# Norms of a two-layer encoder: units around each norm ordered by sequence, mean of squares by a product with ones

## The chip, the cores and the metric

The kernel runs on one core of one Trainium2 chip. The metric is the device time in microseconds of one execution. TensorE does the matrix products, VectorE and ScalarE everything elementwise, GpSimd (POOL) and SyncE issue most of the DMAs. All numbers are float32.

## The reference

Two sequences, of 256 and 512 tokens, go through the same trunk of two layers with 1,024 features; each has its own conditioning vector c. A layer has a mixer and a feed-forward part, and each is fed by a root-mean-square norm that is modulated by c:

```
mod = silu(c) @ w_mod[i] + b_mod[i];  sh1, sc1, g1, sh2, sc2, g2 = split(mod, 6)
h = rmsnorm(x, norm1_g[i]) * (1 + sc1) + sh1
x = x + g1 * mixer(h)              # layer 0: differential attention and gated linear attention; layer 1: mLSTM
h = rmsnorm(x, norm2_g[i]) * (1 + sc2) + sh2
x = x + g2 * ((silu(gate) * up) @ w_down),   gate, up = split(h @ w_gu)
rmsnorm(x, g) = x * rsqrt(mean(x * x) + 1e-6) * g      # mean over the 1,024 features
```

So there are four norms in front of a phase of products (norm 0 before the mixer of layer 0, norm 1 before its feed-forward part, norms 2 and 3 in layer 1) and a last one on the output.

## The kernel before

**Layout.** x, h and all activations lie feature-major: a tile has 128 features in the partitions and 768 columns, the 256 tokens of the first sequence and then the 512 of the second. x has `KD = 8` such tiles. `seq(tile, s)` cuts the columns of sequence s out of a tile: s = 0 is the short one, s = 1 the long one.

**Units.** Every weight matrix is worked off in units of 128 output features (a "feature" unit) or 256 output features with tokens in the partitions (a "token" unit). `plan_units` (L70) puts all units of the kernel in one list; units of one name are a phase. The phases of layer 0 are `bqk0`, `lowrank0`, `bv0`, `aq0`, `ak0`, `bg0`, `av0`, `outb0`, `outa0`, then `gu00`, `down00`, and so on to `down02`; those of layer 1 are `cq1`, `gates1`, `ck1`, `cv1` and `co1`, `out1`, `gu10` to `down12`. The norms stand in front of `bqk0`, `gu00`, `cq1` and `gu10`, behind `outa0` (8 units of 4 k-tiles), `down02` (8 of 6) and `out1` (8 of 8).

**Weights.** Products are made in three parts of a 32-bit operand that is split into a high and a low half: high times high, high times low, low times high. SyncE loads a unit's raw weights into one of four slots as soon as the unit four before it is done (`group_full`); ScalarE copies them to `w_hi` (L1221) and VectorE subtracts to get `w_lo` (L1601). Both do this in `split_to(i)`, which splits all units whose slot was used by a unit up to i. A feature unit is a chain of 3 products per k and per sequence into a pair of banks, 256 columns in the one and 512 in the other (`feature_tile`, L811, products at L824).

**Accumulators.** A pair of banks is free for the next unit when the unit before has been taken out. The phases `gu` and `down` rotate over three pairs, all others over two.

**A norm.** While the phase before runs, VectorE adds each unit's result to x (`residual`, L1737), ScalarE squares the tile (L1278), and VectorE sums the squares (L1667), one tile late. After the last unit TensorE makes the sum over features per token (`norm_sums`, L769): 12 products of the sum and 12 of the last square tile, each with one column of ones, so that tokens lie in the partitions. VectorE scales (L1672, L1673), ScalarE takes the root of 6 columns (L1291), VectorE inverts 6 columns (L1676) and builds six diagonal matrices (L1683), and TensorE broadcasts them over all partitions with a product with ones (L785). Then for each of the 8 tiles and both sequences: `normed` (L1688, VectorE), `h_hi` (L1297, ScalarE), `h_lo` (L1695, VectorE). TensorE runs the first two units of the next phase together, tile by tile as they come (`two_feature_tiles`, L832, products at L842).

**Order.** Each engine's program is one list written by hand; a wait on a semaphore stops all that stands behind it on that engine. At the start, ScalarE copies rows of the modulation out of banks (`mod_row`), splits the first four units, sends x to DRAM (`x_kept`), and goes to norm 0; VectorE splits, completes the modulation of norm 0, makes a table (`band`, L2070) and goes to norm 0. Behind norm 0, VectorE works on further blocks of the modulation (`modulate`, L1617 and L1620, on `early_raw`): GpSimd loads a block when VectorE has freed the buffer of the one two before.

## Time and profile before

| what | value |
| --- | --- |
| three runs | 2117.55, 2123.80, 2126.86 us, median 2123.8 us |
| profiled execution, its own time | 2124.51 us |
| its span, first to last instruction | 2122.4 us |
| mean granted clock of TensorE | 0.967 |
| TensorE busy | 2017.7 us, 95% of the span |
| VectorE busy | 992.6 us, 47% |
| ScalarE busy | 601.7 us, 28% |
| DMA `raw<-in_ffn_w_gu_dram`, 256 KB each | 3.3 us from issue to landing |
| DMA `x_kept<-x`, 3,072 KB each | 10.3 us from issue to landing |

Times are in microseconds from the span's start, durations of single instructions in ns. L824 is line 824 of the kernel. A TensorE instruction's duration holds its way through the array; the spacing of starts is what a product costs. "[3.66 <-DVE h_lo L1695]" means that the engine was idle for 3.66 us before this row and what released it. The granted clock is 1.00 at 2.4 GHz and 0.50 at 1.2 GHz.

### The profile page before, as it was taken

To read this page: it belongs to the slowest core of one execution; us is meant where nothing else is said; L and a number is where in the kernel's file an instruction comes from. 1 tells how busy PE (TensorE), PEld (TensorE's weight loads), DVE (VectorE), ACT (ScalarE), POOL (GpSimd) and SP (SyncE) were. 2 spreads that over 40 slices of the span, in tenths; PEclk is the share of its full clock that TensorE was granted. 3 is DMA by queue.
4 is the path that set the end of the run, shared out by engine and by line. 5 is a ranking of instruction groups with operands and counts; after the bars stand their busy time and mean duration, and the time that the engine had idled before them with its cause. 6 is when DMAs were issued, how large, how long until landed. Compare 5 with 4: busy or idle time off the path is not lost.

```text
span 2122.4 us, 28746 instructions
## 1 busy us (share of the span) xinstructions
PE 2017.7 (95%) x12081; PEld 1742.5 (82%) x12081; DVE 992.6 (47%) x1875; ACT 601.7 (28%) x1101; POOL 74.3 (4%) x121
## 2 busy tenths in 40 slices
PE   7879999988899999999998999998989999999998
PEld 2768888767788888888887788888878888888887
DVE  1877425684766665652235334544452222222224
ACT  3235224652321112211223333334232211211213
POOL 2010000000011101100000000000000000000000
PEclk9889999999899999999998999999989999999999
DMA  7343112012344444432223201021212222222212
GB/s 282 120 150 108 41 41 80 21 31 60 99 142 138 136 122 139 142 96 60 65 62 104 60 20 41 21 99 49 61 50 60 60 70 60 64 66 60 62 56 82
DMA packets 210249, 174.16 MB, mean 82 GB/s; under 512 B 10320, under 2 KB 196792, under 8 KB 208584
## 3 DMA queue, kind: packets, MB, share of 16 engines
q1 hardware_dynamic: 197536, 117.67, 18.5%
q0 software_dynamic: 12288, 48.35, 7.1%
q10 hardware_dynamic: 296, 6.29, 0.7%
q8 instruction: 96, 1.57, 0.3%
q14 instruction: 33, 0.27, 0.0%
HBM read 162.85 MB, written 9.44 MB: 81 GB/s over the span
## 4 chain that ended last, share of the span: by engine, by line
PE 87%; DVE 6%; ACT 4%; issue 2%; DMA 1%; POOL 0%; ACTq 0%; DVEq 0%; POOLq 0%
PE bank L824 60%; PE bank L790 9%; PE bank L842 4%; PE bank L1096 2%; PE bank L747 1%; PE bank L765 1%; DMA early_raw<-in_w_mod_dram 1%; ACT w_hi L1221 1%; DVE early_acc L1620 1%; DVE w_lo L1601 1%; PE bank L1018 1%; PE bank L908 1%; PE bank L1041 1%; PE bank L966 1%; PE bank L1068 1%
## 5 line engine op out<-in xcount | busy, mean ns | idle before, releaser
L824 PE MATMUL bank<-h_hi,w_hi 128*128 128x256 f32 x1600 | 409.4, 338 | 0.1
L824 PE MATMUL bank<-h_lo,w_hi 128*128 128x256 f32 x1600 | 407.5, 336 | 0.0
L824 PE MATMUL bank<-h_hi,w_lo 128*128 128x256 f32 x1600 | 407.3, 336 | 0.0
L1601 DVE TENSOR_TENSOR w_lo<-raw,w_hi 128x1024 fp32r<-128x1024 f32 (+4 forms) x195 | 239.0, 1230 | 340.2 <-ACT w_hi L1221 340.1
L824 PEld LDWEIGHTS bank<-h_hi,w_lo 128*128 128x128 f32 x1600 | 301.3, 188 | 33.6
L824 PEld LDWEIGHTS bank<-h_lo,w_hi 128*128 128x128 f32 x1600 | 301.4, 188 | 33.2
L824 PEld LDWEIGHTS bank<-h_hi,w_hi 128*128 128x128 f32 x1600 | 299.4, 188 | 34.2 <-issue 1.9
L1221 ACT ACTIVATE w_hi<-raw 128x1024 fp32r<-128x1024 f32 (+4 forms) x196 | 205.6, 1053 | 226.3 <-DMA raw<-in_ffn_w_down_dram 129.1
L790 PE MATMUL bank<-w_hi,h_hi 128*128 128x256 f32 x672 | 214.8, 320 | 18.1 <-DVE w_lo L1601 17.7
L790 PE MATMUL bank<-w_lo,h_hi 128*128 128x256 f32 x672 | 195.8, 291 | 0.0
L790 PE MATMUL bank<-w_hi,h_lo 128*128 128x256 f32 x672 | 195.6, 291 | 0.0
L1737 DVE SCALAR_TENSOR_TENSOR x<-bank,mod,x 128x256 f32<-128x256 f32 (+1 forms) x144 | 82.3, 613 | 229.6 <-PE bank L824 225.6
L824 PE MATMUL bank<-act_hi,w_hi 128*128 128x256 f32 x704 | 179.4, 337 | 4.6 <-issue 4.6
L824 PE MATMUL bank<-act_lo,w_hi 128*128 128x256 f32 x704 | 178.8, 336 | 0.0
L824 PE MATMUL bank<-act_hi,w_lo 128*128 128x256 f32 x704 | 178.7, 336 | 0.0
L790 PEld LDWEIGHTS bank<-w_hi,h_hi 128*128 128x128 f32 x672 | 134.5, 200 | 31.0 <-DVE w_lo L1601 18.1
L824 PEld LDWEIGHTS bank<-act_hi,w_hi 128*128 128x128 f32 x704 | 131.7, 188 | 19.8 <-issue 5.8
L824 PEld LDWEIGHTS bank<-act_lo,w_hi 128*128 128x128 f32 x704 | 132.4, 188 | 14.5
L824 PEld LDWEIGHTS bank<-act_hi,w_lo 128*128 128x128 f32 x704 | 132.4, 188 | 14.4
L790 PEld LDWEIGHTS bank<-w_lo,h_hi 128*128 128x128 f32 x672 | 134.6, 200 | 4.9 <-issue 3.8
L790 PEld LDWEIGHTS bank<-w_hi,h_lo 128*128 128x128 f32 x672 | 134.4, 200 | 0.0
L1620 DVE SCALAR_TENSOR_TENSOR late_acc<-late_raw,c_cols,late_acc 128x512 f32<-128x512 f32 x196 | 133.7, 746 | 0.6 <-DMA late_raw<-in_w_mod_dram 0.6
(274 smaller groups left out, 2251.7 us busy)
## 6 DMA issues: line engine op xcount, KB each, us to landing
raw<-in_ffn_w_gu_dram SPq DMA_DIRECT2D x176, 256.0 KB, 3.3
late_raw<-in_w_mod_dram POOLq DMA_DIRECT2D x56, 512.0 KB, 4.3
raw<-in_ffn_w_down_dram SPq DMA_DIRECT2D x64, 256.0 KB, 3.3
early_raw<-in_w_mod_dram POOLq DMA_DIRECT2D x24, 512.0 KB, 4.4
wide<-in_w_mod_dram SPq DMA_DIRECT2D x8, 1024.0 KB, 18.7
raw<-in_odd_w_in_dram SPq DMA_DIRECT2D x16, 512.0 KB, 4.4
raw<-in_even_w_in_dram SPq DMA_DIRECT2D x24, 256.0 KB, 5.0
x_kept<-x ACTq DMA_DIRECT2D x2, 3072.0 KB, 10.3
```

The lines of the kernel that those rows point to most:

```text
L747: last = mm(bank[4 + c][0:2, :], c_cols[:, k, :], wide[k][:, c * 512:(c + 1) * 512], start=(k == 0), stop=(k == KD - 1))
L765: last = mm(mod_column(l, c0 // P + m)[:, s:s + 1], mod_acc(b)[:, s, m * P:(m + 1) * P], ones[:, 0:1], start=True, stop=True)
L790: last = mm(out, stationary[a], moving[b], start=(k == 0 and n == 0), stop=(k == K - 1 and n == 2))
L824: last = mm(pair(u.pair)[s], wk[a], seq(operand(o, k), s), start=(k == 0 and n == 0), stop=(k == u.ks - 1 and n == 2))
L842: last = mm(pair(u.pair)[s], wk[a], seq(operand(o, k), s), start=(k == 0 and n == 0), stop=(k == u.ks - 1 and n == 2))
L908: last = transpose(out[s][:, c:c + P], source(t), ident[:])
L966: last = mm(bank[6][:, d * P:(d + 1) * P], k_e[c][rows, t * P:(t + 1) * P], q_e[c][rows, t * P:(t + 1) * P], start=True, stop=True)
L1096: last = mm(bank[7][:, 0:C_V + 1], weights[d][:, c:c + P], z_cv[:, h, i, :], start=(i == froms[0]), stop=(i == froms[-1]))
L1221: fn(hi, r, ACT.Copy).then_inc(hi_ready, 1)
L1601: v.tensor_tensor(lo, r, hi.bitcast(F32), ALU.subtract).then_inc(unit_split, 1)
L1620: ins = v.scalar_tensor_tensor(acc, mod_raw(m)[:, kk, :], c, acc, ALU.mult, ALU.add)
L1737: last = v.scalar_tensor_tensor(seq(x[:, f, :], s), pair(u.pair)[s], mod[l][:, gate + f, s:s + 1], seq(x[:, f, :], s), ALU.mult, ALU.add)
```

## The change

At norms 1 to 3 the last two units of the phase before (`TAILS`) are worked off by sequence: the long sequence of unit 6 and of unit 7, the short one of unit 6, the sums for the long one, the short one of unit 7. At norms 0 to 3 the first three units of the phase behind (`HEADS`) are: the long sequence of units 0 and 1 together, tile by tile, with the sums for the short one behind the third tile, the long one of unit 2, and then the short one of units 0, 1 and 2. The three have a pair of banks each.

The sum over features is made with the 128 x 128 matrix of ones as the stationary operand and the squares as the moving one, three products for each sequence (the sum of the first six tiles, and the squares of the last two). Each partition then holds the sums of all tokens, in a bank. ScalarE takes the root of mean plus epsilon over the whole row out of the bank into `rstd_all`, VectorE inverts the row in place. The diagonal matrices and their 12 products go, and so do the sums per token, except at the last norm, which stays as it was.

`normed`, `h_hi` and `h_lo` run over the 8 tiles of the long sequence and then over those of the short one. Between them stand, on VectorE, the short residual of unit 7, the two weight splits and the second inversion; on ScalarE, the last square, the second root and two weight splits, and at norms 0 and 2 the DMA of x to DRAM. At norm 0 the sums are made before `turn_rows`, and ScalarE takes both roots ahead of its first weight splits.

The diff, cut to its core:

```diff
-        rstd_diag = at("rstd_diag", Z + 57 * KB, [P, TILES, P])
+        rstd_all = at("rstd_all", Z + 57 * KB, [P, T])
...
+        TAILS = ("outa0", f"down0{FG - 1}", "out1")
+        HEADS = ("bqk0", "gu00", "cq1", "gu10")
...
-            pairs = 3 if base in ("gu", "down") else 2
-            u.pair = (0 if u.n == 0 and pairs == 3 else features) % pairs
+            if u.tail is not None:
+                by = "res"
+                taken["res"] = 4 * u.tail + 2 + u.n - (KD - 2)
+            pairs = 3 if base in ("gu", "down") or u.name in HEADS and u.n < 3 else 2
+            u.pair = u.n if u.name in HEADS and u.n < 3 else (0 if u.n == 0 and pairs == 3 else features) % pairs
...
-        def mean_bank(n):
-
-            return bank[6 if 0 < n < 4 else 0]
+        def mean_of(n, s):
+
+            if n == 0:
+                return pair(0)[s]
+            return bank[6][:] if s else bank[7][:, 256:512]
...
-            def norm_sums(n):
-
-                pe.wait_ge(sq_summed, (KD - 2) * (n + 1))
+            def norm_sums(n, s):
+
+                pe.wait_ge(sq_summed, (KD - 3) * (n + 1))
+                if n == 0:
+                    pe.wait_ge(tr_free, KD)
+                mm(mean_of(n, s), ones[:], seq(square_sum, s), start=True, stop=False)
+                for f in (KD - 2, KD - 1):
+                    pe.wait_ge(sq_ready, 10 * n + (7, 9)[1 - s] + f - (KD - 2))
+                    last = mm(mean_of(n, s), ones[:], seq(square[f % 2], s), start=False, stop=(f == KD - 1))
+                last.then_inc(mean_full, 1)
...
-                for t in range(TILES):
-                    s = SEQ_OF_TILE[t]
-                    c = (t - SEQ_TILES[s][0]) * P
-                    pe.wait_ge(rdiag_ready, TILES * n + t + 1)
-                    mm(pair(2)[s][:, c:c + P], ones[:], rstd_diag[:, t, :], start=True, stop=True).then_inc(rstd_full, 1)
...
+            def tail_units(us, n, operand):
+
+                for u in us:
+                    pe.wait_ge(unit_split, u.i + 1)
+                    wait_free(u)
+                for s in (1, 0):
+                    for u in us:
+                        if s == 0 and u is us[1]:
+                            if n == 2:
+                                pe.wait_ge(mod_ready, 1 + len(MOD_BLOCKS))
+                            norm_sums(n, 1)
+                        for k in range(u.ks):
+                            wk = [slot_of(wt, u)[:, k * P:(k + 1) * P] for wt in (w_hi, w_lo)]
+                            for m, (a, o) in enumerate(((0, 0), (0, 1), (1, 0))):
+                                last = mm(pair(u.pair)[s], wk[a], seq(operand(o, k), s),
+                                          start=(k == 0 and m == 0), stop=(k == u.ks - 1 and m == 2))
+                        last.then_inc(group_full, 1)
+
+            def head_units(us, n):
+
+                def products(u, s, k):
+                    wk = [slot_of(wt, u)[:, k * P:(k + 1) * P] for wt in (w_hi, w_lo)]
+                    for m, (a, o) in enumerate(((0, 0), (0, 1), (1, 0))):
+                        last = mm(pair(u.pair)[s], wk[a], seq(normal(o, k), s),
+                                  start=(k == 0 and m == 0), stop=(k == KD - 1 and m == 2))
+                    return last
+
+                for u in us[:2]:
+                    pe.wait_ge(unit_split, u.i + 1)
+                    wait_free(u)
+                for k in range(KD):
+                    pe.wait_ge(h_ready, 2 * KD * n + k + 1)
+                    for u in us[:2]:
+                        products(u, 1, k)
+                    if n and k == 2:
+                        norm_sums(n, 0)
+                pe.wait_ge(unit_split, us[2].i + 1)
+                wait_free(us[2])
+                for k in range(KD):
+                    products(us[2], 1, k)
+                for u in us:
+                    for k in range(KD):
+                        if u is us[0]:
+                            pe.wait_ge(h_ready, 2 * KD * n + KD + k + 1)
+                        last = products(u, 0, k)
+                    last.then_inc(group_full, 1)
+                for u in us:
+                    after(u)
...
+            pe.wait_ge(row_taken, 4)
+            norm_sums(0, 1)
+            norm_sums(0, 0)
...
+            def mean_root(n, s):
+
+                act.wait_ge(mean_full, 2 * n + 2 - s)
+                fn(seq(rstd_all, s), mean_of(n, s), ACT.Sqrt, scale=1.0 / D, bias=eps_col[:, 0:1]).then_inc(root_ready, 1)
+
             def norm(n, i):
-                act.wait_ge(mean_ready, n + 1)
+
+                def high(f, s):
+                    act.wait_ge(normed_ready, 2 * KD * n + KD * (1 - s) + f + 1)
+                    fn(seq(h_hi[:, f, :], s), seq(normed[f % 2], s), ACT.Identity,
+                       bias=mod[n // 2][:, (SH1, SH2)[i] + f, s:s + 1]).then_inc(h_hi_ready, 1)
+
+                def square_late(f, s, done):
+                    act.wait_ge(res_done, 4 * (n - 1) + done)
+                    square_part(n, f, s)
+
+                if n:
+                    us = phase[TAILS[n - 1]]
+                    split_to(us[KD - 3].i)
+                    fn(dummy[:], ones[:, 0:1], ACT.Sqrt)
+                    square_late(KD - 2, 1, 1)
+                    square_late(KD - 1, 1, 2)
+                    square_late(KD - 2, 0, 3)
+                    mean_root(n, 1)
+                for f in range(KD):
+                    high(f, 1)
+                    if n and f == 1:
+                        square_late(KD - 1, 0, 4)
+                    if n and f == 3:
+                        mean_root(n, 0)
+                        split_to(us[KD - 2].i)
+                if n:
+                    split_to(us[KD - 1].i)
+                if n % 2 == 0:
+                    spill()
+                for f in range(KD):
+                    high(f, 0)
...
+            for s in (1, 0):
+                for q in (KD - 2, KD - 1):
+                    square_part(0, q, s)
             act.wait_ge(mod_full, KD)
             for c in (0, 1):
                 fn(mod_row[:, c * 512:(c + 1) * 512], bank[4 + c][0:2, :], ACT.Copy).then_inc(row_taken, 1)
+            mean_root(0, 1)
+            mean_root(0, 0)
...
+            def inverse(n, s):
+
+                dve.wait_ge(root_ready, 2 * n + 2 - s)
+                link(v.reciprocal(seq(rstd_all, s), seq(rstd_all, s)))
+
+            def norm(n, l, i, gate=None, gate_l=None):
+
+                before = 2 * KD * n
+
+                def part_residual(u, s):
+                    dve.wait_ge(group_full, u.full[s])
+                    v.scalar_tensor_tensor(seq(x[:, u.n, :], s), pair(u.pair)[s], mod[gate_l][:, gate + u.n, s:s + 1],
+                                           seq(x[:, u.n, :], s), ALU.mult, ALU.add).then_inc(res_done, 1)
+
+                def scaled(f, s):
+                    if f >= 2:
+                        dve.wait_ge(h_ready, before + KD * (1 - s) + f - 1)
+                    v.scalar_tensor_tensor(seq(normed[f % 2], s), seq(x[:, f, :], s), gain[l][i][:, f, s:s + 1],
+                                           seq(rstd_all, s), ALU.mult, ALU.mult).then_inc(normed_ready, 1)
+
+                def rest(f, s):
+                    dve.wait_ge(h_hi_ready, before + KD * (1 - s) + f + 1)
+                    v.scalar_tensor_tensor(seq(h_lo[:, f, :], s), seq(normed[f % 2], s),
+                                           mod[l][:, (SH1, SH2)[i] + f, s:s + 1],
+                                           seq(h_hi[:, f, :], s).bitcast(F32), ALU.add, ALU.subtract).then_inc(h_ready, 1)
+
+                dve.wait_ge(mod_ready, (1, 1 + EARLY // MOD_PARTS, 1 + len(MOD_BLOCKS), 1 + len(MOD_BLOCKS))[n])
+                if n:
+                    us = phase[TAILS[n - 1]]
+                    add_squares(n, KD - 3)
+                    split_to(us[KD - 3].i)
+                    part_residual(us[KD - 2], 1)
+                    part_residual(us[KD - 1], 1)
+                    part_residual(us[KD - 2], 0)
+                    inverse(n, 1)
                 for f in range(KD):
-                    if f >= 2:
-                        dve.wait_ge(h_ready, h_before[l, i] + f - 1)
-                    scaled(f)
-                    if f >= 1:
-                        rest(f - 1)
-                rest(KD - 1)
+                    if f == 0:
+                        scaled(0, 1)
+                    if f + 1 < KD:
+                        scaled(f + 1, 1)
+                    rest(f, 1)
+                    if n and f == 0:
+                        part_residual(us[KD - 1], 0)
+                    if n and f == 4:
+                        split_to(us[KD - 2].i)
+                if n:
+                    inverse(n, 0)
+                for f in range(KD):
+                    if f == 0:
+                        scaled(0, 0)
+                    if f + 1 < KD:
+                        scaled(f + 1, 0)
+                    rest(f, 0)
+                    if n and f == 1:
+                        split_to(us[KD - 1].i)
...
+            inverse(0, 1)
+            inverse(0, 0)
             norm(0, 0, 0)
```

## Rows read from the trace of the kernel before

**Rows 1.** The page, busy time of each engine:

```profile
PE 2017.7 (95%) x12081; PEld 1742.5 (82%) x12081; DVE 992.6 (47%) x1875; ACT 601.7 (28%) x1101; POOL 74.3 (4%) x121
```

**Rows 2.** Waits of TensorE: us in total, times, longest:

```profile
PE bank L790 <- DVE w_lo L1601: 17.7, 2, 12.6
...
PE bank L842 <- DVE x L1737: 1.4, 1, 1.4
```

**Rows 3.** Timeline at the fourth norm: start, us, engine, line, operation, idle before:

```profile
1539.87 1.14 DVE L1737 SCALAR_TENSOR_TENSOR x<-bank,mod,x 128x256 f32<-128x256 f32 x2 [3.38 <-PE bank L824]
...
1547.64 2.19 DVE L1688 SCALAR_TENSOR_TENSOR normed<-x,gain,bank 128x256 f32<-128x256 f32 x4 [2.04 <-PE bank L785]
...
1551.27 0.98 PE L842 MATMUL bank<-h_hi,w_hi 128*128 128x256 f32 x2 [3.66 <-DVE h_lo L1695]
```

**Rows 4.** Windows: stretch, busy PE PEld DVE ACT POOL, granted clock, DMA:

```profile
1552.00:1556.00 4.00, 4.00 (x14) 3.37 (x13) 3.93 (x8) 2.24 (x4) 0.00 (x0) 0.50 0.00 0
```

**Rows 5.** Timeline, takers of the units that bound the fourth, third and second norm:

```profile
1522.91 1.14 DVE L1737 SCALAR_TENSOR_TENSOR x<-bank,mod,x 128x256 f32<-128x256 f32 x2 [3.38 <-PE bank L824]
...
1579.12 0.88 ACT L1322 ACTIVATE silu_g<-bank 128x256 f32<-128x256 f32 x2 [3.47 <-PE bank L824]
...
1111.80 1.14 DVE L1737 SCALAR_TENSOR_TENSOR x<-bank,mod,x 128x256 f32<-128x256 f32 x2 [1.62 <-PE bank L824]
...
1164.23 0.87 ACT L1254 ACTIVATE z_o<-bank 128x256 f32<-128x256 f32 x2 [6.65 <-PE bank L824]
...
521.75 1.14 DVE L1737 SCALAR_TENSOR_TENSOR x<-bank,mod,x 128x256 f32<-128x256 f32 x2
...
562.86 0.38 ACT L1322 ACTIVATE silu_g<-bank 128x256 f32<-128x256 f32 x1 [2.86 <-PE bank L842]
```

**Rows 6.** Timeline of TensorE, two spacings of products and the plain f32 ones:

```profile
1530.24 0.40 PE L824 MATMUL bank<-odd_hi,w_hi 128*128 128x512 f32 x1
...
1530.47 0.52 PE L824 MATMUL bank<-odd_lo,w_hi 128*128 128x256 f32 x2
...
42.51 7.03 PE L747 MATMUL bank<-wide,c_cols 128*2 128x512 f32 x16
```

**Rows 7.** Groups by form: count, busy us, mean ns, idle before:

```profile
L1688 DVE SCALAR_TENSOR_TENSOR normed<-x,gain,bank 128x512 f32<-128x512 f32 x32 | 23.8, 742 | 0.0
...
L1601 DVE TENSOR_TENSOR w_lo<-raw,w_hi 128x1024 fp32r<-128x1024 f32 x148 | 180.4, 1223 | 268.8 <-ACT w_hi L1221 268.8
...
L1297 ACT ACTIVATE h_hi<-normed,mod 128x512 fp32r<-128x512 f32 x32 | 22.7, 708 | 0.0
```

**Rows 8.** Groups by form, the reciprocals of VectorE:

```profile
L1868 DVE RECIPROCAL recip<-denom 128x2 f32<-128x2 f32 x24 | 3.8, 159 | 0.0
...
L1676 DVE RECIPROCAL mean_sq<-mean_sq 128x6 f32<-128x6 f32 x5 | 1.0, 192 | 1.4 <-ACT mean_sq L1291 1.4
...
L1716 DVE RECIPROCAL rstd<-rstd 128x24 f32<-128x24 f32 x1 | 0.3, 304 | 0.9 <-ACT rstd L1303 0.9
```

**Rows 9.** Windows, an idle spell and what follows it:

```profile
1484.00:1488.00 4.00, 0.83 (x5) 0.75 (x6) 2.15 (x3) 2.73 (x3) 0.00 (x0) 1.00 0.92 251
...
1488.00:1492.00 4.00, 4.00 (x16) 3.43 (x15) 2.15 (x4) 1.79 (x2) 0.00 (x0) 0.59 0.05 14
```

**Rows 10.** Timeline at the first norm and up to the token unit:

```profile
50.55 3.88 ACT L1221 ACTIVATE w_hi<-raw 128x1024 fp32r<-128x1024 f32 x4
...
50.91 1.32 PE L754 MATMUL bank<-ident,mod_row 2*128 2x2 f32 x16 [1.37 <-DVE mod_row L2064]
...
57.46 1.09 DVE L2070 SCALAR_TENSOR_TENSOR band<-band 128x896 f32<-128x896 f32 x1
...
62.76 2.19 DVE L1688 SCALAR_TENSOR_TENSOR normed<-x,gain,bank 128x256 f32<-128x256 f32 x4 [2.05 <-PE bank L785]
...
80.84 0.88 DVE L1617 TENSOR_SCALAR early_acc<-early_raw,c_cols 128x512 f32<-128x512 f32 x2
...
125.27 2.28 DVE L1601 TENSOR_TENSOR w_lo<-raw,w_hi 128x2048 fp32r<-128x2048 f32 x1
```

More of the change, by code:

```diff
@@ L859, in feature_units @@
+            def feature_units(name, before=None, operand=normal, mix=None, head=None, tail=None):
                 us = phase[name]
+                if head is not None:
+                    head_units(us[:3], head)
+                    us = us[3:]
                 if before:
@@ L1548, in _ @@
             run(phase["outb0"], take_nothing, mix)
[L1549 removed]
+            run(phase["outa0"][:-2], squares_of(1), mix)
             norm(1, 1)
             feed_forward(0)
[L1552 removed]
             norm(2, 0)
```

157 lines of the change are left out of this document (71 added, 86 removed).

## The prediction

> **What bounds the kernel now.** I read the page's first part first: TensorE is busy for 95% of the span, so the time is the products plus the few places where they stop [rows 1]. Second the waits of TensorE: the longest single one, 12.6 us, is not at a norm at all but at the first token unit of the even layer, for a `w_lo` of VectorE; a second row shows what two accumulator pairs cost when a pass needs both free at its start, 1.4 us [rows 2]. Third the timeline around one norm (the fourth, before `gu10`). VectorE takes up the last unit at 1539.87; the sums, the root, the diagonal and the broadcast products follow, `normed` starts at 1547.64, and the first product of the next phase at 1551.27. The products ended 0.2 us before VectorE started, so the gap is 1551.27 - 1539.67 = 11.6 us [rows 3]. Fourth the clock by windows: half (1.2 of 2.4 GHz) at 1552 to 1556, with TensorE busy again [rows 4]. It stayed so for some 5.5 us of products, worth about 2.5 us.
>
> I measure a norm from the end of unit 5 of the phase before (the third last) to the end of unit 2 (the third) of the phase behind, since all that is moved lies between. Each end is 0.2 us before the row of its taker. Last norm: 1522.91 to 1579.12, 56.2 us. Third: 1111.80 to 1164.23, 52.4. Second: 521.75 to 562.86 for unit 0, and then one k of unit 1 (1.1) and unit 2 (8.5) less the taker's 0.2, 50.5 [rows 5].
>
> **Unit prices.** A product of 512 columns takes 0.235 us (1530.24 to 1530.47, rounded), and units 6 and 7 of `out1` took (1539.87 - 1522.91) / 48 = 0.353 for a pair of 256 and 512 [rows 3, 5], so 256 take 0.12. I take it that the parts cost no more when ordered by sequence, since each product is an instruction of its own already; the bound the other way, 512 columns at 0.26, would cost 1 us a norm. The sums' operands are plain f32: 16 of 512 columns in 7.03 us, 0.43 each [rows 6]. VectorE: 0.74 us for 512 columns; an `x` of 256 and 512 takes 1.14 [rows 3], so 256 alone about 0.48; two in a row without a wait overlap by 0.08; a split of a unit 1.22. ScalarE: 0.71 for an `h_hi` of 512; for the root of 512 out of a bank I take 0.65 [rows 7].
>
> **The new operation: a reciprocal over whole rows.** `rstd` is now taken in every partition, and VectorE inverts 512 and 256 columns at each norm where it inverted 6. The trace has no wide one. Two columns take 159 ns, six 192, 24 take 304 [rows 8]. From 6 to 24 that is 6.2 ns a column: 0.30 + 488 x 0.0062 = 3.34 us for 512, and 1.75 for 256. Upper bound, the slope from 2 to 6, 8.2 ns: 4.3 and 2.2. Lower bound: as fast as any other 512 (0.74 and 0.48). I take the first, as it is the same instruction over the widest step, and 18 more columns at the pace of the 512s could have cost only 0.02 us. It speaks against the change either way. The Trainium skill (VectorE: DVE Perf Modes, "First, the fixed hardware budget") says that reciprocal is an iterative divide "with a repeat count of 8". If that is eight steps a column at the pace of the 512 rows (1.03 ns), it would be about 4.4 and 2.3 us, an estimate by that page, and the sum below would end at 2133; the row of 24 columns bears out six steps, the one of six columns eight.
>
> **Last norm, step by step** (from the end of unit 5 as 0). The pass over units 6 and 7 asks for both accumulators at its start, and unit 7's belongs to unit 5: the 1.4 us of [rows 2], new here and at the second norm; the third has three pairs and none. Long sequence of unit 6 (24 x 0.235) to 7.0, of unit 7 to 12.7, short one of unit 6 to 15.6, three sums to 16.9, short one of unit 7 to 19.7. Beside it: VectorE adds unit 7's long part to x from 12.9, ScalarE squares it by 14.3, so the sums don't wait. Root from 17.1 to 17.7, reciprocal to 21.1, `normed` 0.74, `h_hi` 0.71, `h_lo` 0.74 with their handovers to 23.4. The first two units ask for both pairs at their start, and unit 7's short residual (0.5) stands behind the first `h_lo` on VectorE, so the first product is at 24.0. The gap is 4.3 us instead of 11.6, and 24 small sums and 12 broadcast products are gone.
> Then the head. VectorE's period for the long sequence is 0.74 - 0.08 + 0.74 + 0.03 = 1.44 us a k, and TensorE's for two units 6 x 0.235 = 1.41: with nothing to spare, all that VectorE and ScalarE do in between is paid. Besides that residual it is the root of the short sequence, for which ScalarE waits on sums that TensorE issues behind k = 2, and then a `w_hi` of 1.05, which make `h_hi` 4 late by about 1.7, and the `w_lo` split behind `h_lo` 4 (1.2). TensorE idles 3.1 us in k 1 to 7 and, with its sums (0.65), ends the long pass at 39.0. Unit 2's long part to 44.7. VectorE meanwhile inverts the short sequence (1.75) and runs 8 periods of 0.91 with a split; TensorE waits 0.5 for it, and unit 2 ends at 53.9. So 29.9 us from the first product; before it was 27.6 of which 2.5 clock. Total 53.9 for 56.2: 2.3 gained.
> Third norm: tail 14.1 (short tiles of 6), gap 5.0, head 29.9: 48.9 for 52.4, 3.5 gained. Second: tail 11.5 with the stall, gap 5.7 (the last short part of 4 k hides less), head 29.9: 47.0 for 50.5, 3.5 gained.
>
> **Clock.** Idle spells of some 3 us in this trace are followed by a few us at half clock: the window 1484 to 1488 has 0.83 us of products, and 1488 to 1492 has a granted clock of 0.59, 1.7 us lost [rows 9]. Each new gap is of that size. In the head 1.7 us of loss is partly eaten by TensorE's later waits on VectorE; stepping through it, 1.2 stay. The waits inside the head may bring a second such spell: a half chance of 1.2, 0.6. So 1.8 a norm. The three norms gain 9.3 - 5.4 = 3.9 us (bounds: 9.3 without any loss, about -1 where both spells come in full at each, 3.4 a norm).
>
> **First norm.** Nothing precedes it but the row copies, so only losses are in reach. ScalarE's root now stands ahead of its four weight splits. TensorE starts the six sums at 50.9, when the rows are copied; 1.95 us at full clock, 3.3 with most at half, and with handover and root ScalarE is free at about 54.9, where its splits began at 50.55 [rows 10]: 4.3 later, and VectorE's splits with them. VectorE's band work ended at 58.55 and `normed` began at 62.76, 4.2 us; now two reciprocals stand there, 5.2: 1.0. The eight k took 18.2 us to 80.9; now 8 x 1.44 + 8 x 0.91 with the start, 20.2: 2.1. Sum 7.4, say 7.5. TensorE's own path would lose about 4, but it doesn't set the end: behind the norm VectorE runs its modulation blocks from 80.84 in one chain, each needing the buffers the last one freed, up to the `w_lo` that ends at 127.55, for which TensorE waits 12.6 us [rows 2, 10]. All of the 7.5 is passed on. Bounds: 3.6 (reciprocal cheap) to 9. The spill of x (10.3 us to land by the page) moves behind the long pass, is issued at about 80 and lands before unit 0 is full at about 93: nothing, with 2 us of cover.
>
> **Sum.** 2124.5 (profiled execution; 0.7 above the median of the three runs) + 7.5 - 3.9 = 2128.1, on the median's scale 2127.
>
> **Rivals.**
> A, wide reciprocal as cheap as any other 512: the first norm costs 3.6, the others gain 3.1 more each (2.6 at the gap, 0.5 in the short pass), 13.2: 2124.5 + 3.6 - 13.2 = 2115, 2114 on the median's scale. The slope speaks against it.
> B, no clock loss: each gap is under half of the old one and the granted clock stays at 1: 9.3 - 7.5, 2122. Rows 9 speak against it, but such spells are few.
> C, slower: the head starved by VectorE. TensorE waits k by k in the long pass, and the clock falls twice per norm: once with the 2.5 us of the old gap, once more with 1.4. That is 3.9 against the 3.1 gained, 0.8 lost at each of three norms: 2124.5 + 7.5 + 2.4 = 2134. It decides as soon as two half-clock spells follow one norm. For it: 1.44 against 1.41. Against: TensorE never rests over 2 us at a time inside the head.
> D, reciprocal at the steeper slope: 1.0 and 0.5 more at each of four norms, 6 in all: 2133. The row of 24 columns is against it. (It is what the page of the Trainium skill named above would give.)
> E, the first norm's delay is taken up by the 12.6 us wait, if that wait has another cause (the DMA of the modulation blocks running on its own time): only TensorE's 4, 2124.
>
> **Chances.** Forecast (2124 to 2131) 0.45, A 0.11, B 0.14, C 0.11, D 0.09, E 0.10. Half a per cent is 10.6 us and is about what a measurement of this kernel can tell: under 2113 is A with some luck, 0.14; over 2134 is C, or C with D, 0.16; 0.70 within. Range 2114 to 2137: A's centre to C and D together.
>
> **What would show it.** `RECIPROCAL rstd_all` of 512 at 3.3 us (A: 0.7, D: 4.4). First product of `gu10` 24 us after unit 5's end, unit 2's end 54 to 55.5 after it. `h_hi` 4 late by a `w_hi` at every norm but the first. The first modulation block at about 88.3 instead of 80.84, and the first L790 product at about 135 instead of 127.6. It would be wrong if the 12.6 us wait shrinks by the delay, if the clock stays full through the gaps, or if the tail's both-accumulators stall isn't there.

## The result, and the profile after

| | before | after |
| --- | --- | --- |
| median of the timed runs | 2124.08 us (5 runs, 2117.55 to 2126.86) | 2136.57 us (5 runs, 2133.82 to 2140.5) |
| profiled execution, its span | 2124.51, 2122.4 us | 2133.82, 2132.1 us |
| mean granted clock | 0.967 | 0.976 |

The ratio is 1.006, 95% interval 1.0039 to 1.008. Ten more runs of the changed kernel gave 1.0043 (1.0022 to 1.0064). So the change costs 9 to 13 us; forecast were 3. The five runs before were on the quick side: 31 later runs of the same kernel have a median of 2127.99 us. The page of the changed kernel, busy time of each engine, stands against [rows 1]:

```profile
PE 2010.2 (94%) x11985; PEld 1722.7 (81%) x11985; DVE 1005.0 (47%) x1844; ACT 609.8 (29%) x1113; POOL 74.3 (3%) x121
```

TensorE is busy for 7.5 us less and still ends later. The waits of TensorE (us in total, times, longest) answer to [rows 2]:

```profile
PE bank L894 <- DVE h_lo L1811: 21.9, 7, 15.0
PE bank L808 <- DVE w_lo L1712: 15.9, 2, 10.9
PE bank L894 <- DVE x L1800: 14.5, 3, 5.5
```

L894 holds the head's products, L808 the token units'. "Long" and "short" stand for the sequences of 512 and of 256 tokens, a "taker" is the first instruction on VectorE or ScalarE that reads a finished unit out of its banks, and tiles are counted from 0, so that `h_lo` 4 is the fifth. The token unit still waits 10.9 us for `w_lo`, 1.7 less than before, of a delay of 7.7. The groups by form on VectorE (count, busy us, mean ns, idle before) have the new operation, against [rows 8]:

```profile
L1792 DVE RECIPROCAL rstd_all<-rstd_all 128x512 f32<-128x512 f32 x4 | 13.4, 3353 | 8.5 <-ACT rstd_all L1372 8.4
...
L1792 DVE RECIPROCAL rstd_all<-rstd_all 128x256 f32<-128x256 f32 x4 | 7.0, 1747 | 0.0
```

The timeline of the changed kernel at the first norm, against [rows 10]:

```profile
53.35 0.69 ACT L1372 ACTIVATE rstd_all<-bank,eps_col 128x512 f32<-128x512 f32 x1 [1.85 <-PE bank L791]
...
54.64 0.47 ACT L1372 ACTIVATE rstd_all<-bank,eps_col 128x256 f32<-128x256 f32 x1 [0.61 <-PE bank L791]
55.02 3.88 ACT L1292 ACTIVATE w_hi<-raw 128x1024 fp32r<-128x1024 f32 x4
...
61.93 1.09 DVE L2208 SCALAR_TENSOR_TENSOR band<-band 128x896 f32<-128x896 f32 x1
63.05 5.14 DVE L1792 RECIPROCAL rstd_all<-rstd_all 128x512 f32<-128x512 f32 x2
68.23 1.42 DVE L1806 SCALAR_TENSOR_TENSOR normed<-x,gain,rstd_all 128x512 f32<-128x512 f32 x2
...
135.29 0.58 PE L808 MATMUL bank<-w_hi,h_hi 128*128 128x256 f32 x1 [10.85 <-DVE w_lo L1712]
```

ScalarE's splits start at 55.02 instead of 50.55, `band` ends at 63.02 instead of 58.55, the inversions take 5.14, and the first token product comes at 135.3 where it came at 127.6.

The timeline of the changed kernel at the fourth norm, against [rows 3]; unit 5 ends at 1528.63:

```profile
1530.12 0.47 PE L885 MATMUL bank<-odd_hi,w_hi 128*128 128x512 f32 x1 [1.33 <-DVE x L1874]
...
1543.98 1.02 PE L788 MATMUL bank<-square_sum,ones 128*128 128x512 f32 x2
1544.84 1.88 PE L791 MATMUL bank<-square,ones 128*128 128x512 f32 x4
1546.15 0.68 PE L885 MATMUL bank<-odd_hi,w_hi 128*128 128x256 f32 x1
...
1547.47 3.35 DVE L1792 RECIPROCAL rstd_all<-rstd_all 128x512 f32<-128x512 f32 x1 [2.81 <-ACT rstd_all L1372]
...
1553.65 0.77 PE L894 MATMUL bank<-h_hi,w_hi 128*128 128x512 f32 x1 [4.07 <-DVE x L1800]
...
1556.78 0.63 PE L894 MATMUL bank<-h_lo,w_hi 128*128 128x512 f32 x1
1557.20 0.63 PE L894 MATMUL bank<-h_hi,w_lo 128*128 128x512 f32 x1
...
1560.44 0.59 PE L788 MATMUL bank<-square_sum,ones 128*128 128x256 f32 x2
...
1561.93 0.47 ACT L1372 ACTIVATE rstd_all<-bank,eps_col 128x256 f32<-128x256 f32 x1 [5.51 <-PE bank L791]
...
1563.99 0.75 DVE L1811 SCALAR_TENSOR_TENSOR h_lo<-normed,mod,h_hi 128x512 fp32r<-128x512 f32 x1 [5.43 <-ACT h_hi L1378]
```

Read it from below. VectorE stands for 5.43 us before the fifth `h_lo`. It waits for ScalarE, which stands 5.51 us before the short root. That waits for TensorE's short sums at 1560.44. They stand behind three tiles of products, and TensorE comes to them 6.8 us after the first head product (1553.65), since its products of 512 columns start 0.42 apart here (1556.78, 1557.20) and not 0.235. The windows of the changed kernel (columns as in rows 4) show it, with a granted clock of 0.55 and 0.60 up to the sums and of 1.00 behind them:

```profile
1552.00:1556.00 4.00, 2.35 (x6) 1.90 (x7) 3.84 (x7) 2.48 (x5) 0.00 (x0) 0.55 0.19 56
1556.00:1560.00 4.00, 4.00 (x13) 3.16 (x12) 2.49 (x4) 0.42 (x1) 0.00 (x0) 0.60 0.02 4
1560.00:1564.00 4.00, 3.28 (x15) 2.44 (x13) 0.01 (x1) 2.07 (x4) 0.00 (x0) 1.00 0.00 0
```

The rows of the sums show one thing more. The program asks for three products (one of `square_sum`, two of `square`), and the trace has six records: a product with plain f32 operands leaves two (L747 has 64 records in the kernel before, for the 32 products that the program asks for). Six records at 0.43 us (0.86 for the first two, 1543.98 to 1544.84) are 2.6 us, and the short sums take half of that, 1.3 us. So the 24 small sums and 12 broadcasts of a norm that stand above as products are records too; the kernel before has 12 and 6 products.

From unit 5's end, in us, at norms 1, 2 and 3 (before: 50.5, 52.4 and 56.2 in all):

| norm | first head product | from there to the end of unit 2 | in all | VectorE's wait before `h_lo` 4 |
| --- | --- | --- | --- | --- |
| 1 | 18.15 | 31.7 | 49.9 | 4.58 |
| 2 | 20.19 | 31.6 | 51.8 | 4.62 |
| 3 | 25.02 | 32.6 | 57.6 | 5.43 |

**Where the 9.7 us between the two spans are.** First norm, up to the first token product: +7.7. The three norms: -0.6, -0.6, +1.4. The stages between: +1.8, with both signs in them, from -4.2 in the odd layer's mixer to +5.9 in the feed-forward part of layer 0 (norm 1's unit 2 to unit 5 of `down02`); in the latter the slow pace of 576 to 695 and from 911 us on, told below, is worth about 6. No instruction was added there. The takers of the `gu1` units show what changed. The timeline of ScalarE in the kernel before:

```profile
1629.05 0.88 ACT L1322 ACTIVATE silu_g<-bank 128x256 f32<-128x256 f32 x2 [5.41 <-PE bank L824]
1645.68 0.88 ACT L1322 ACTIVATE silu_g<-bank 128x256 f32<-128x256 f32 x2 [5.41 <-PE bank L824]
```

and in the changed one:

```profile
1620.36 0.87 ACT L1432 ACTIVATE silu_g<-bank 128x256 f32<-128x256 f32 x2 [5.57 <-PE bank L842]
1637.32 0.87 ACT L1432 ACTIVATE silu_g<-bank 128x256 f32<-128x256 f32 x2 [5.57 <-PE bank L842]
```

Two units, 48 pairs of 256 and 512 columns, take 16.63 us before and 16.96 after, at a granted clock of 1.00 in both; by the starts of TensorE's products that is 0.3467 and 0.3533 us a pair. These are two paces of one instruction stream; over all pairs, the excess over 0.3467 (called the excess from here on) adds up to 3.5 us in the profile before and 10.2 in the one after. The experiments ask whether that belongs to the change.

### The profile page after: what moved, and what is told of

It is laid out like the page before. It is cut to its first block and busy times, and to the rows that moved or that the text cites. A ratio compares the mean times of both kernels' runs of the same rounds, so it can differ in the third digit from the quotient of the medians.

```text
span 2132.1 us, 28543 instructions
## 1 busy us (share of the span) xinstructions
PE 2010.2 (94%) x11985; PEld 1722.7 (81%) x11985; DVE 1005.0 (47%) x1844; ACT 609.8 (29%) x1113; POOL 74.3 (3%) x121
## 5 line engine op out<-in xcount | busy, mean ns | idle before, releaser
L842 PE MATMUL bank<-h_hi,w_hi 128*128 128x256 f32 (+1 forms) x1536 | 395.6, 339 | 0.2 <-ACT z_bv L1333 0.2
L842 PE MATMUL bank<-h_hi,w_lo 128*128 128x256 f32 (+1 forms) x1536 | 395.2, 339 | 0.0
L842 PE MATMUL bank<-h_lo,w_hi 128*128 128x256 f32 (+1 forms) x1536 | 395.0, 339 | 0.0
L842 PEld LDWEIGHTS bank<-h_hi,w_lo 128*128 128x128 f32 x1536 | 290.4, 189 | 34.4
L842 PEld LDWEIGHTS bank<-h_lo,w_hi 128*128 128x128 f32 x1536 | 290.6, 189 | 32.7
L842 PEld LDWEIGHTS bank<-h_hi,w_hi 128*128 128x128 f32 x1536 | 288.8, 189 | 34.3 <-issue 1.4
L808 PE MATMUL bank<-w_hi,h_hi 128*128 128x256 f32 x672 | 212.5, 316 | 16.4 <-DVE w_lo L1712 15.9
L808 PE MATMUL bank<-w_lo,h_hi 128*128 128x256 f32 x672 | 193.9, 288 | 0.0
L808 PE MATMUL bank<-w_hi,h_lo 128*128 128x256 f32 x672 | 193.5, 288 | 0.0
L842 PE MATMUL bank<-act_hi,w_hi 128*128 128x256 f32 (+1 forms) x680 | 174.5, 338 | 4.6 <-issue 4.6
L842 PE MATMUL bank<-act_hi,w_lo 128*128 128x256 f32 (+1 forms) x680 | 174.0, 338 | 0.0
L842 PE MATMUL bank<-act_lo,w_hi 128*128 128x256 f32 (+1 forms) x680 | 172.7, 336 | 0.0
L808 PEld LDWEIGHTS bank<-w_hi,h_hi 128*128 128x128 f32 x672 | 132.3, 197 | 28.9 <-DVE w_lo L1712 16.3
L808 PEld LDWEIGHTS bank<-w_lo,h_hi 128*128 128x128 f32 x672 | 132.4, 197 | 4.8 <-issue 3.8
L1436 ACT ACTIVATE act_hi<-prod 128x768 fp32r<-128x768 f32 x44 | 37.2, 846 | 335.2 <-DVE prod L1894 335.2
```

The source lines that it names most:

```text
L808: last = mm(out, stationary[a], moving[b], start=(k == 0 and n == 0), stop=(k == K - 1 and n == 2))
L842: last = mm(pair(u.pair)[s], wk[a], seq(operand(o, k), s), start=(k == 0 and n == 0), stop=(k == u.ks - 1 and n == 2))
L1436: fn(act_hi[:, j, :], prod[:], ACT.Copy).then_inc(act_hi_ready, 1)
```

## The experiments

The theory at this point had four parts: (1) which pace holds is drawn anew each time TensorE starts again, and that explains the scatter of the runs; (2) the first norm's loss is the roots ahead of the splits; (3) the norms' loss is the short root, which waits for sums that TensorE reaches late at half clock; (4) the inversion costs its full length at each norm. All ratios are to the kernel before on the same chip, with 95% intervals; the intervals reach about 0.2%, 4 us, to either side, so a smaller difference between two variants can be read from the traces alone.

**The changed kernel once more.** No edit.

> The changed kernel, unaltered, for a second profile. In the first profile the pair of a 256- and a 512-column product in the feed-forward part of layer 0 starts every 0.3533 us in 577 to 696 and again in 911 to 1122, and every 0.3467 in between, while the kernel before has 0.3467 throughout; that accounts for about 5.9 us of the 9.3 between the two profiled executions. Theory 1 (the pace is drawn anew each time TensorE starts after an idle spell): this profile has the slow pace in other phases than the first, and the time moves by up to 10 us with it. Theory 2 (the pace belongs to the order of the program): the same phases are slow within a few us. Ratio to the kernel before 1.004 to 1.008 either way.

1.0043 (1.0022 to 1.0064). First token product 135.7, norms 49.7, 51.8, 56.4, waits before `h_lo` 4 of 4.4, 4.6, 4.2: the same. The pace was slow in other stretches (fast from 918 to 1177 us, slow from 500 to 918), as the first theory has it. The excess was 9.6 us in all against 10.2, and yet the span was 2.3 us longer (2134.4), so the pace isn't the whole of the scatter.

**Roots of the first norm behind the splits.**

```diff
-            mean_root(0, 1)
-            mean_root(0, 0)
             split_to(-1)
+            mean_root(0, 1)
+            mean_root(0, 0)
```

> At norm 0 alone ScalarE takes its two roots behind the four weight splits instead of ahead of them. Theory (norm 0's delay is passed on whole through VectorE's chain of modulation blocks): the band work ends 4.3 us earlier, the first modulation block starts at about 83.4 instead of 87.65 and the first token product at about 131 instead of 135.3: 4 us less than the changed kernel. Rival (the chain runs on the DMA of the blocks): the first token product stays within 1 us of 135.3 and the time is unchanged.

The timeline of this kernel:

```profile
50.61 3.88 ACT L1292 ACTIVATE w_hi<-raw 128x1024 fp32r<-128x1024 f32 x4
55.80 1.05 ACT L1372 ACTIVATE rstd_all<-bank,eps_col 128x512 f32<-128x512 f32 x2
...
58.64 5.14 DVE L1792 RECIPROCAL rstd_all<-rstd_all 128x512 f32<-128x512 f32 x2
...
129.94 0.58 PE L808 MATMUL bank<-w_hi,h_hi 128*128 128x256 f32 x1 [13.30 <-DVE w_lo L1712]
```

The splits are back at 50.6 and the token product comes 5.35 us sooner: part 2 holds in the trace, and the wait for `w_lo` is 13.3 us, so it hides next to nothing of a delay. The ratio did not move: 1.0042 (1.0023 to 1.006). In the profile the gain is still there at unit 5 before the fourth norm (1522.9 against 1528.6) and gone at the end (span 2135.6): the slow pace held to the end, where the changed kernel's first profile was fast from 1699 us on, which is worth 8 of the 9 us. The excess was 18.2 us in all. Whether that was so in most of the ten runs is not known.

**Short root and split two tiles later.**

```diff
-                    if n and f == 3:
+                    if n and f == 5:
                         mean_root(n, 0)
```

(and VectorE's split behind `h_lo` 6 instead of 4)

> At norms 1 to 3 ScalarE's root of the short sequence and the weight split behind it move from behind the fourth h_hi to behind the sixth, VectorE's split from behind the fifth h_lo to behind the seventh. Theory (ScalarE waited for sums that TensorE reached late at half clock, 4.6 to 5.4 us of VectorE's idle time before the fifth h_lo at each norm): that wait goes to under 0.5 us, and from the first product of the head to the end of its third unit it takes 29 to 30 us instead of 31.7 to 32.6: 2 to 3 us a norm, 6 to 9 in all. Rival (TensorE at half clock is itself the limit of the head, the wait only reflects it): the wait moves to h_lo 7, and under 1 us a norm is gained.

1.0009 (0.9982 to 1.0036). Norms 48.0, 49.5, 54.6; the first head products where they were (18.16, 20.18, 25.01). 7.1 us gained behind them, as part 3 says. But the wait was expected to fall under 0.5 us, and 2.4 to 2.8 stay, now before `h_lo` 6. The timeline names what it is:

```profile
1551.46 0.59 PE L788 MATMUL bank<-square_sum,ones 128*128 128x256 f32 x2
...
1552.96 0.47 ACT L1372 ACTIVATE rstd_all<-bank,eps_col 128x256 f32<-128x256 f32 x1 [2.64 <-PE bank L791]
...
1555.02 0.75 DVE L1811 SCALAR_TENSOR_TENSOR h_lo<-normed,mod,h_hi 128x512 fp32r<-128x512 f32 x1 [2.56 <-ACT h_hi L1378]
```

**The same, and TensorE's short sums one tile sooner.**

```diff
-                    if n and k == 2:
+                    if n and k == 1:
                         norm_sums(n, 0)
```

> The short root and the weight split behind h_hi 5 and 6 of the long sequence, as in the run that placed them late, and the short sequence's sums after k = 1 of the head instead of k = 2. Theory (what is left of the wait before h_lo 6, 2.4 to 2.8 us, is TensorE at half clock reaching the sums: two units by three products by 0.43 us for each k): the sums come 2.6 us earlier, the wait before h_lo falls under 0.6 us at each norm, and the norms are 1 to 2.5 us shorter than with the late root alone (48.0, 49.5, 54.6 us): 46 to 47, 47 to 48.5 and 52.5 to 53.5; the time 2124 to 2129. Rival (the wait is the root's table or the residual's square, not TensorE's place): the wait stays at 2 to 3 us and the time at 2130.

1.0003 (0.9986 to 1.0021), norms 46.3, 48.2, 52.8. The timeline of this kernel at norm 1, and at norm 3 with no idle time before the root:

```profile
552.84 0.75 DVE L1811 SCALAR_TENSOR_TENSOR h_lo<-normed,mod,h_hi 128x512 fp32r<-128x512 f32 x1 [0.36 <-ACT h_hi L1378]
...
1553.31 0.59 PE L788 MATMUL bank<-square_sum,ones 128*128 128x256 f32 x2
...
1554.80 0.48 ACT L1372 ACTIVATE rstd_all<-bank,eps_col 128x256 f32<-128x256 f32 x1
```

No wait over 0.4 us is left before an `h_lo`. So the wait, and what it costs, are shown: two moves, with no work taken away, bring 11 to 12 us of the norms (147.3 in all three, against 159.3 and 157.9 in the two profiles of the changed kernel). By the ratios the time fell by 0.4% of the changed kernel's, some 8 us (median 2130.6, where 2124 to 2129 were expected). The 4.9 us of the second move don't show in the time (1.0009 and 1.0003), and the intervals are too wide to tell.

**Without the inversion.** `reciprocal` becomes a multiplication by 0.02 of the same shape; the norm is then not computed, so this is a bound and no version.

> The inversion of the root over whole rows is left out at norms 0 to 3: a multiplication by a constant of the same shape stands in its place (the norm is not computed any more). Theory: 3.35 and 1.75 us become about 0.5 and 0.3, so norm 0 ends 4.3 us earlier on VectorE and passes that on to the first token product (131 instead of 135.3), and each other norm gains 2.8 at the gap and up to 1 behind: 12 to 15 us less than the changed kernel, ratio to the kernel before 0.999 to 1.001. Rival (the head is bound by its own products and waits): under 6 us in all.

0.9958 (0.9937 to 0.9978), 18 us under the changed kernel. In its timeline the operation takes 0.43 us:

```profile
1534.84 0.43 DVE L1792 TENSOR_SCALAR rstd_all<-rstd_all 128x512 f32<-128x512 f32 x1 [2.81 <-ACT rstd_all L1372]
```

This kernel also settles how much of the wait before `h_lo` 4 is the clock's. At its fourth norm TensorE ran at full clock (granted clock 1.00 from 1536 to 1544), with the short sums still behind the third tile:

```profile
1538.10 0.47 PE L894 MATMUL bank<-h_hi,w_hi 128*128 128x512 f32 x1 [1.15 <-DVE x L1800]
...
1542.29 0.59 PE L788 MATMUL bank<-square_sum,ones 128*128 128x256 f32 x2
...
1545.85 0.75 DVE L1811 SCALAR_TENSOR_TENSOR h_lo<-normed,mod,h_hi 128x512 fp32r<-128x512 f32 x1 [2.84 <-ACT h_hi L1378]
```

The sums come 4.2 us behind the first head product and the wait is 2.84. In the changed kernel they come 5.9, 5.8 and 6.8 behind it, and the waits are 4.58, 4.62 and 5.43 (4.38, 4.58 and 4.18 in its second profile). At the other two norms of this kernel the granted clock was 0.73 and 0.72 up to the sums and the waits 4.26 and 4.61, so leaving out the inversion doesn't shorten them. Part 3 as it stood is half of the truth: the place behind three tiles makes 2.8 us of the wait at full clock, and the half clock adds 1.3 to 2.6.

Each first head product comes 2.9 us sooner (15.19, 17.27, 22.11), the first token product at 130.3 (5.0 sooner), the norms take 46.0, 48.3, 51.5. Part 4 holds. The time fell by more than the 12 to 15 us expected; the trace adds up to 18.5, in which the full clock at the fourth norm has its share.

**The order alone.** Sums per token, narrow root and reciprocal, diagonals and broadcast products as before the change; the order by sequence stays, and the first norm's roots stand behind the splits.

```diff
-                link(v.reciprocal(seq(rstd_all, s), seq(rstd_all, s)))
+                link(v.reciprocal(mean_sq[:, ts[0]:ts[-1] + 1], mean_sq[:, ts[0]:ts[-1] + 1]))
+                for t in ts:
+                    v.tensor_scalar(rstd_diag[:, t, :], ident[:], mean_sq[:, t:t + 1], None, ALU.mult).then_inc(rdiag_ready, 1)
```

> The first half of the change alone: the order by sequence stays, the second half is undone (sums per token in single columns, a root over 4 or 2 columns, a reciprocal over 4 or 2 columns, diagonals, and products of ones with the diagonals, issued after the sixth k of the tail's last unit and after k = 1 of the head's third unit; at the first norm the roots stand behind the four weight splits, as before the change). Theory (at norms 1 to 3 the two forms cost about the same, since what the long reciprocal takes on VectorE, 3.35 us, the narrow form takes in 24 weight loads of 0.12, 2.9 against 2.2 us, four diagonals, 0.8, and eight broadcast products, 2.0; the second half costs time at the first norm alone): modulation starts at 81 to 83 us and the first token product at 128 to 130 (135.3 with the change); the three norms 49 to 52, 51 to 54 and 56 to 59 us, the wait before h_lo 4 at 5 to 7 us, since the short sums at half clock are 12 weight loads of 0.22 (2.6 us) against 1.6; the time 2127 to 2134, some 5 under the changed kernel's 2136. Rival (the second half eats the order's gain at the norms too): each of the three norms 3 to 4 us shorter than the changed kernel's, 46, 48 and 53 us, and the time 2116 to 2122.

1.0052 (1.0024 to 1.008), 2140.16: outside what either side expected. First token product 131.8 (not 128 to 130: TensorE now makes the single-column sums, 7.2 us of them mostly at half clock, ahead of the row transposes that VectorE needs). Norms 52.9, 53.6, 59.2, all longer than the changed kernel's. The timeline at norm 3:

```profile
1556.11 0.18 DVE L1822 RECIPROCAL mean_sq<-mean_sq 128x4 f32<-128x4 f32 x1 [2.39 <-ACT mean_sq L1401]
1556.33 0.88 DVE L1824 TENSOR_SCALAR rstd_diag<-ident,mean_sq 128x128 f32<-128x128 f32 x4
...
1558.68 1.80 PE L814 MATMUL bank<-rstd_diag,ones 128*128 128x128 f32 x8
...
1581.94 0.87 DVE L1840 SCALAR_TENSOR_TENSOR normed<-x,gain,bank 128x256 f32<-128x256 f32 x2 [3.43 <-PE bank L814]
```

The narrow inversion saves 3 us on VectorE, and the diagonals, the wait for the place in TensorE's list and four products (eight records) take them back: the first head products come at 18.2, 20.1 and 25.6 us, where the changed kernel has 18.15, 20.19 and 25.02. All that is longer lies behind them; for the short sequence VectorE waits 3.43 us for broadcasts that I had placed behind the third unit's second k. That wait is a mistake of placement in this kernel, not of the form. What can be said: the wide form isn't what makes the norms of the changed kernel slow. The expectation that the two forms cost about the same holds up to the first head product; that the placement alone makes the rest longer is argued and not shown. The ten runs spread from 2131.2 to 2153.7 us, and the profiled one is the slowest.

**Last unit of the attention tails in a third pair of banks.**

```diff
+            if u.tail is not None and u.n == KD - 1 and base != "down":
+                u.pair = 2
```

> The changed kernel with the last unit of the two attention stages (out of norms 1 and 3) in the third pair of banks instead of the second, so that the last two units don't wait for the residual of unit 5. Theory (the stall of 1.4 us at the start of the last two units, seen twice, is on the path): both stalls go, the first head product of norms 1 and 3 comes 1.2 to 1.5 us sooner after unit 5's end (16.8 and 23.6 us against 18.15 and 25.0), the norms are 48.4 and 56.2 us against 49.9 and 57.6, the middle one stays at 51.8, and the time falls by 2 to 4 to 2132 to 2134. Rival (the head waits for VectorE's long pass over the square, the root and the reciprocal, which start from the last residual anyway): the stalls go, and the first head product comes no sooner, or comes sooner by under 0.5 us; the time stays at 2136.

1.0026 (1.0003 to 1.0049). The wait of 1.33 in the timeline at the fourth norm above is gone, the first head products come at 16.99 and 23.08 (1.2 and 1.9 sooner), norm 2 is unchanged at 20.20. The norms take 49.1, 51.8 and 54.8 us, and the stall was on the path. The time doesn't show it: 2137.2 where 2132 to 2134 were expected, and the ratio is within the interval of the changed kernel's.

**The kernel before once more.** No edit.

> The kernel before, unaltered, for a second profile of it. Theory 1 (TensorE takes one of two paces for a pair of 256 and 512 columns, 0.3467 or 0.3533 us, drawn anew whenever it starts again after an idle spell, the same for both kernels): its first profile held the slow pace after the third norm only (3.5 us in all); this one should hold it in other stretches, between 0 and 18 us in all, and its span should move with that sum. Rival (each kernel has its paces fixed by its own order of work): slow again from 1140 us on and nowhere else, 3 to 4 us in all. The first norm (modulation at 80.8, first token product at 127.6) and the three norms (50.5, 52.4, 56.2 us from unit 5's end to the third unit's end) repeat to 0.7 us, but for the spells at half clock, by either.

Span 2128.8, 6.4 us over its first profile; the first norm was the same (modulation at 80.90, token product at 127.5), and the excess over the fast pace was 10.0 instead of 3.5, 6.5 us more. The timeline of ScalarE in it, two neighbouring takers of `gu0` units, with two units and the sums of a modulation block between them:

```profile
775.18 0.88 ACT L1322 ACTIVATE silu_g<-bank 128x256 f32<-128x256 f32 x2 [13.67 <-PE bank L824]
793.92 0.88 ACT L1322 ACTIVATE silu_g<-bank 128x256 f32<-128x256 f32 x2 [7.35 <-PE bank L824]
```

and in its first profile:

```profile
769.21 0.88 ACT L1322 ACTIVATE silu_g<-bank 128x256 f32<-128x256 f32 x2 [13.52 <-PE bank L824]
787.64 0.88 ACT L1322 ACTIVATE silu_g<-bank 128x256 f32<-128x256 f32 x2 [7.20 <-PE bank L824]
```

18.74 and 18.43 us for the same work of the same kernel. The excess went up by what the span did. So the pace is no property of the program alone, and that much of part 1 holds; that the whole scatter comes of it isn't shown. Nor is it free of the program. Behind norms 1 and 3 (600 to 680 and 1610 to 1680 us) it was fast in both profiles of the kernel before and slow in all eight with the new head taken up to then.

**All four moves together.**

> The changed kernel with all four placements: the first norm's roots behind the four weight splits, the short root and split behind h_hi 5 and 6, the short sums after k = 1 of the head, the attention tails' last unit in the third pair of banks. Theory (the four act in different places and add up in the trace): modulation starts at 83 us and the first token product comes at 130; the norms take 45 to 46, 48 to 48.5 and 49.5 to 51 us, without a wait over 0.6 us before h_lo; the stretches behind the first and third head run at the slow pace of TensorE; the time 2117 to 2124, 6 to 13 under the kernel before. Rival (what the first norm gives back doesn't arrive, as in the run that moved the roots alone, because the stages behind it give it up again): 2125 to 2130, with the trace's gain of 5 us at the first token product gone by the end of unit 5 before the second norm, 392 us later.

0.9962 (0.9942 to 0.9981), median 2120.39 (12 runs, 2114.69 to 2125.45): the fastest of those that compute the norm, 8 to 10 us under the kernel before and, by the ratios, 17 under the changed one. In its profile the first token product came at 131.9 and the norms took 45.6, 48.7 and 51.0, with no wait over 0.84 before an `h_lo`: 3.4 and 14.0 us under the changed kernel's, 17.4 together, as the times say. Whether what the first norm gives back arrives isn't settled: in the profile, which is the slowest of the twelve runs, 0.9 of the 3.4 us are left at unit 5 before norm 1 (526.1 against 527.0), and its span is 8.4 under the changed kernel's.

**The same with the wide product first** in every feature unit outside heads and tails.

```diff
-                        for s in range(2):
+                        for s in (1, 0):
```

> The same kernel with the long sequence's product (512 columns) ahead of the short one's (256) in every feature unit outside heads and tails. In eight profiles with the head ordered by sequence the stretches behind the first and the third head (600 to 680 and 1610 to 1680 us) ran at 0.3533 us for a pair, in both profiles of the kernel before at 0.3467, and the stage between (1190 to 1400) at the slow pace for 0.5 to 0.76 of it against none. Theory (the pace there follows from how the alternating pairs start behind a run of 256-column products, the head's last three blocks): with the wide product first these stretches show 0.3467 us, and the time is 3 to 6 us under the same kernel without the swap. Rival (the pace has to do with when TensorE last started, not with the order): the stretches stay at 0.3533 and the time is the same within 2 us, or the whole kernel takes another pace still.

0.9966 (0.9946 to 0.9985), median 2123.90. Behind norm 1 the pace was fast for the first time with this head, behind norm 3 slow (takers 16.96 apart), the excess 20.1 us against 13.1. Neither side held; one profile can't tell a share from a draw. Why the new head is followed by the slow pace stays open.

## Why the prediction came out as it did

The time of 2136.6 lay just inside the range of 2114 to 2137 and on its slow edge, 9.6 over the forecast. Between the two spans the first norm is 7.7 of 9.7 us (forecast 7.5), the norms 0.2 (forecast -3.9) and the stages between 1.8 (forecast nothing). That the time stayed inside the range is in part luck, since the largest single piece, the pace, is in no step. Step by step:

- **The reciprocal**: 3.34 and 1.75 forecast, 3.353 and 1.747 measured. The slope between 6 and 24 columns carried over to 512. A and D fall. The Trainium skill's count of 8 (VectorE: DVE Perf Modes, "First, the fixed hardware budget") doesn't fit these rows if it is read as eight steps a column, as I did: (3353 - 1747) / 256 is 6.3 ns a column, six steps of 1.03 ns.
- **First norm**: +7.5 forecast; measured +6.8 at the start of the modulation (87.65) and +7.7 at the first token product. By its three terms: splits 4.5 (4.3), inversion 5.2 against 4.2 (the same), passes 19.4 from `normed` to the modulation (20.2). The 4.3 came out by two errors that cancel: I had the six sums at 1.95 us, 3.3 at half clock, and they took 3.9 at a granted clock of 1.00. E falls: the wait of 12.6 shrank by 1.7 only, and with the roots moved back it was 13.3.
- **The price of a sum** is the term that was mis-sized most. I read rows 6 as 16 products at 0.43 us. They are 16 records of eight products, 0.86 each, so the long sums take 2.6 us where I had 1.3 and the short ones 1.3 where I had 0.65. The first head products came at 18.15, 20.19 and 25.02, where I had 17.2, 19.1 and 24.0: 3 of the 4.1 us that the norms missed by. The tail's stall was there (1.33) and on the path, and the gap was 4.1 for 4.3 forecast.
- **The wait inside the head** was mis-sized too: "make `h_hi` 4 late by about 1.7". VectorE waited 4.6, 4.6 and 5.4 us. Of that 2.8 is the place of the sums behind three tiles, at full clock and at their true price; the rest is the half clock, which I had as a cost to TensorE's own products only, "in the head 1.7 us of loss is partly eaten by TensorE's later waits". It also makes the sums late, and with them ScalarE's root and all that VectorE has behind it.
- **The head's length** came out all the same. With the 1.8 us of clock it was forecast at 31.7, and it took 31.7, 31.6 and 32.6. The larger wait lay beside TensorE's slow products: TensorE itself stood for 2.3 us in each head (1.52 and 0.80), where I had 3.1. So this term was right by two errors, and it hid what there was to gain: taking the wait away made the norms 11 to 12 us shorter.
- **Clock**: one spell at half clock a norm, so rival C's second one didn't come. Over the whole kernel there was less of it: by the mean granted clocks of 0.967 and 0.976, some 140 us at half clock before and 102 after.
- **What no step had**: the pace. By the profiles 6.7 of the 9.7 us between the spans are in it, and it hid a gain of the odd stage (-4.2, fewer half-clock windows). Part of it is chance (the kernel before shows 3.5 and 10.0), part goes with the new head, and why is open.

## What to carry to other kernels

A small operation that one engine issues in the midst of a stream, and on whose result two others wait in order, is to be priced with the slowest clock of the stream ahead of it, and placed as early as its inputs allow while its consumer is placed as late as its need allows: here that was worth 11 to 12 us in the trace and some 8 in the time, for no work removed. Ahead of a chain that runs with nothing to spare (1.44 against 1.41 us a tile) most of such a wait is paid: without the 4.6, 4.6 and 5.4 us the norms were 3.6, 3.6 and 4.8 shorter. A price read from a row is the price of a record; count the records against the products that the program asks for. And a difference of 5 us between two profiles of a 2,100 us kernel is no evidence before the spacing of its products is compared in stretches that the change doesn't touch.

## What the runs showed that I had not expected

At a granted clock of 1.00, pairs of products of 256 and 512 columns come either 0.3467 or 0.3533 us apart, 1.9% between them, never in between over a stretch, and most switches lie where TensorE starts again after a stop or goes from one kind of unit to another. The twelve profiles show 3.5 to 20.1 us of excess in 2,130. That is somewhat less than the scatter of the timed runs (2117.6 to 2143.5 for the kernel before); how much of the scatter it makes isn't shown.
